# The first layer's modulation in five column blocks instead of four, with a half-width block at either end

## What is computed

```python
sc = jax.nn.silu(c)                 # latent tokens
scc = jax.nn.silu(c_ctx)            # context tokens
mod = sc @ ada_w + ada_b            # ada_w is 2048 x 6144
shift, scale, gate = jnp.split(mod[:, None, :], 3, axis=-1)
mod_c = scc @ ada_w + ada_b
h = rms_norm(x, norm_w) * (1 + scale) + shift
hc = rms_norm(ctx, norm_w) * (1 + scale_c) + shift_c
q, k, v, z = jnp.split(t @ w_in, 4, axis=-1)      # t is h, then hc; w_in is 2048 x 8192
```

## Time and profile before

| | us |
|---|---|
| median of 3 runs | 2140.7 (2139.47 to 2143.54) |
| the profiled execution's own time | 2139.08 |
| its span | 2137.5 |
| TensorE busy | 2049.5 (96%) |
| VectorE busy | 1438.1 (67%) |
| ScalarE busy | 913.5 |
| GpSimd busy | 776.6 |

### The profile page before, as it was taken

One profiled execution on the slowest core, in us unless ns is written; L12 is line 12 of the kernel. 1 busy time (PEld: TensorE's weight loads), 2 busy tenths in 40 slices (PEclk: granted clock), 3 DMA queues, 4 the chain that ended last, 5 costly groups with the idle time before them and its releaser, 6 DMA issues.

```text
span 2137.5 us, 31164 instructions
## 1 busy us (share of the span) xinstructions
PE 2049.5 (96%) x10694; PEld 1695.5 (79%) x10694; DVE 1438.1 (67%) x1865; ACT 913.5 (43%) x1259; POOL 776.6 (36%) x687
## 2 busy tenths in 40 slices
PE   5989999999999999989988999999999999999997
PEld 2558888888888888768867888888888888887776
DVE  5257777777787777744267767677767667678344
ACT  3244445444455455533354433433443434435433
POOL 1126666666665565645041221221322222222011
PEclk7999999999999999999989999999999999999999
DMA  9976666666676666445434455455454555544653
GB/s 352 361 218 143 184 162 170 171 175 176 174 189 171 169 174 171 137 133 152 111 106 123 127 138 148 118 137 149 106 162 113 142 141 134 127 133 167 239 194 138
DMA packets 417744, 349.21 MB, mean 163 GB/s; under 512 B 13504, under 2 KB 358176, under 8 KB 416544
## 3 DMA queue, kind: packets, MB, share of 16 engines
q1 hardware_dynamic: 392304, 269.76, 43.7%
q0 software_dynamic: 20400, 74.46, 13.8%
q10 hardware_dynamic: 4992, 4.37, 0.7%
HBM read 344.21 MB, written 4.33 MB: 163 GB/s over the span
## 4 chain that ended last, share of the span: by engine, by line
PE 84%; DVE 7%; DMA 3%; ACT 2%; issue 2%; POOL 0%; SPq 0%; DVEq 0%; POOLq 0%; ACTq 0%
PE bank L357 21%; PE bank L361 21%; PE bank L359 21%; PE bank L2104 2%; PE bank L2106 2%; PE bank L2105 2%; PE bank L2034 2%; DMA arena<-in_na_ada_w_dram 2%; DVE w_lo L343 2%; PE bank L2017 1%; PE bank L2027 1%; DVE act_lo L1513 1%; PE bank L1836 1%; PE bank L1810 1%; PE bank L1895 1%
## 5 line engine op out<-in xcount | busy, mean ns | idle before, releaser
L357 PE MATMUL bank<-act_hi,w_hi 128*128 128x512 f32 (+1 forms) x2480 | 916.6, 370 | 22.3 <-DVE w_lo L343 12.3
L361 PE MATMUL bank<-act_hi,w_lo 128*128 128x512 f32 (+1 forms) x2480 | 901.0, 363 | 0.0
L359 PE MATMUL bank<-act_lo,w_hi 128*128 128x512 f32 (+1 forms) x2480 | 900.9, 363 | 0.0
L343 DVE TENSOR_TENSOR w_lo<-arena,w_hi 128x2048 fp32r<-128x2048 f32 x186 | 441.7, 2375 | 182.7 <-ACT w_hi L339 132.7
L357 PEld LDWEIGHTS bank<-act_hi,w_hi 128*128 128x128 f32 x2480 | 471.1, 190 | 100.7 <-DVE w_lo L343 11.6
L361 PEld LDWEIGHTS bank<-act_hi,w_lo 128*128 128x128 f32 x2480 | 470.5, 190 | 73.8
L359 PEld LDWEIGHTS bank<-act_lo,w_hi 128*128 128x128 f32 x2480 | 471.4, 190 | 69.1
L581 POOL TENSOR_TENSOR acc<-acc,arena 128x512 f32<-128x512 f32 x224 | 334.1, 1492 | 123.0 <-ACT arena L830 113.9
L339 ACT ACTIVATE w_hi<-arena 128x2048 fp32r<-128x2048 f32 x141 | 269.2, 1909 | 97.7 <-PE bank L2106 78.2
L1316 DVE SCALAR_TENSOR_TENSOR arena<-arena,cond_c 128x512 f32<-128x512 f32 x240 | 253.3, 1056 | 72.8 <-DMA arena<-in_ssd_ada_w_dram 48.3
L830 ACT ACTIVATE arena<-arena,cond_c 128x512 f32<-128x512 f32 x256 | 171.3, 720 | 283.8 <-POOL acc L581 153.2
(11 more groups left out here) (247 smaller groups left out, 2123.4 us busy)
## 6 DMA issues: line engine op xcount, KB each, us to landing
arena<-in_ssd_w_in_dram SPq DMA_DIRECT2D x81, 1024.0 KB, 6.0
arena<-in_na_w_in_dram SPq DMA_DIRECT2D x58, 1024.0 KB, 7.2
arena<-in_ssd_ada_w_dram POOLq DMA_DIRECT2D x96, 512.0 KB, 4.1
arena<-in_na_ada_w_dram SPq DMA_DIRECT2D x64, 512.0 KB, 8.6
arena<-in_ssd_w_out_dram SPq DMA_DIRECT2D x32, 1024.0 KB, 5.0
arena<-in_na_ada_w_dram POOLq DMA_DIRECT2D x32, 512.0 KB, 4.1
arena<-in_na_w_out_dram SPq DMA_DIRECT2D x16, 1024.0 KB, 6.4
arena<-cs_scr SPq DMA_DIRECT2D x64, 256.0 KB, 5.3
```

The source lines that it names most:

```text
L343: nc.vector.tensor_tensor(w_lo[:, n0 % 2, :], raw[slot], w_hi[:, n0 % 2, :].bitcast(F32), ALU.subtract).then_inc(s_lo, 1)
L357: nc.tensor.matmul(bank[b][:, 0:cols], w_hi[:, b, w], act_hi3[:, k, 0:cols], start=(k == 0), stop=False)
L359: nc.tensor.matmul(bank[b][:, 0:cols], w_hi[:, b, w], act_lo3[:, k, 0:cols], start=False, stop=False)
L361: mm = nc.tensor.matmul(bank[b][:, 0:cols], w_lo[:, b, w], act_hi3[:, k, 0:cols], start=False, stop=(k == KT - 1))
```

## The change

The columns are taken in five blocks, given as first feature tile and number of tiles in `BLOCKS`: two tiles (256 columns), three times four, two. There are 40 steps instead of 32; those of the first and last block are two loads of 256 KB, in the same four slots. The weight groups keep their size and are loaded after q = 3 and q = 7 of the first four blocks; the last block has none among its steps.

The norm's row goes to bank 1 and is copied once to SBUF (`x_rows`); VectorE multiplies it onto tiles 0 and 1, and onto the other 14 only after the first block's `h`. The waits of the first block ask for two tiles only.

In TensorE's order the last block takes its first five steps before the first piece of the block ahead (`q >= 4 if c == 4`), three pieces come behind `mod_columns(4)`, and only four pieces are left at the end.

```diff
+BLOCKS = ((0, 2), (2, 4), (6, 4), (10, 4), (14, 2))
...
+            for c_block, (k0, kn) in enumerate(BLOCKS):
+                for q in range(8):
+                    n = 8 * c_block + q
+                    if n >= 4:
+                        sp.wait_ge(s_ada_used, n - 3)
+                    for b in range(2):
+                        sp.dma_start(ada_slot[n % 4][:, :, b, 0:P * kn],
+                                     ada_rows[:, 2 * q:2 * q + 2, b * D + P * k0:b * D + P * (k0 + kn)])\
+                          .then_inc(s_ada[n % 4], 16)
+                    if c_block < 4 and q % 4 == 3:
+                        load_first_weights(2 * c_block + q // 4)
...
-            pool.wait_ge(s_xn0, KT)
...
-            for k in range(KT):
-                nc.vector.tensor_tensor(xn_t[:, k, :], bank[3][:, :], xn_t[:, k, :], ALU.mult).then_inc(s_xn0, 1)
+
+            def x_normed(k0, k1):
+                for k in range(k0, k1):
+                    nc.vector.tensor_tensor(xn_t[:, k, :], x_rows, xn_t[:, k, :], ALU.mult).then_inc(s_xn0, 1)
+
+            step(nc.vector.tensor_copy(x_rows, bank[1][:, :]))
+            step.wait()
+            x_normed(0, BLOCKS[0][1])
...
+                if c == 0:
+                    x_normed(k0 + kn, KT)
...
-            for c in range(4):
+            for c in range(len(BLOCKS)):
+                pieces = [] if c == 0 else list(range(2 * BLOCKS[c - 1][1]))
                 for q in range(8):
                     mod_products(c, q)
                     if c == 0 and q == 2:
                         norm_rows()
-                    if c > 0 and q >= 2:
-                        first_tiles(c - 1, q - 2)
-                if c > 0:
-                    first_tiles(c - 1, 6)
+                    if q >= (4 if c == 4 else 2) and pieces:
+                        first_tiles(c - 1, pieces.pop(0))
+                if pieces:
+                    first_tiles(c - 1, pieces.pop(0))
                 mod_columns(c)
-                if c > 0:
-                    first_tiles(c - 1, 7)
-            for p in range(8):
-                first_tiles(3, p)
+                for p in pieces:
+                    first_tiles(c - 1, p)
+            for p in range(2 * BLOCKS[4][1]):
+                first_tiles(4, p)
```

More of the change, by code:

```diff
@@ L583, in _ @@
             for k in range(KT):
-                if k % 4 == 0:
-                    pool.wait_ge(s_mod, k // 4 + 1)
-                if k == KT - 4:
+                for c_block, (k0, kn) in enumerate(BLOCKS):
+                    if k == k0:
+                        pool.wait_ge(s_mod, c_block + 1)
+                        pool.wait_ge(s_xn0, k0 + kn if c_block == 0 else KT)
+                if k == BLOCKS[-1][0]:
                     load_ada(0, None, True)
@@ L788, in _ @@
             act.sem_inc(s_hi, PRE)
-            for c in range(4):
+            for c, (k0, kn) in enumerate(BLOCKS):
                 act.wait_ge(s_ada_used, 8 * (c + 1))
@@ L792, in _ @@
                     act.wait_ge(s_rtr, c)
-                nc.scalar.activation(rows_a[:, c % 2, :], bank[2][:, :], ACT.Copy).then_inc(s_rows, 1)
-                first_hi(2 * c)
+                nc.scalar.activation(rows_a[:, c % 2, 0:P * kn], bank[2][:, 0:P * kn], ACT.Copy).then_inc(s_rows, 1)
+                first_hi(k0 // 2)
                 act.wait_ge(s_mod, c + 1)
-                act.wait_ge(s_xn0, KT)
-                for k in range(4 * c, 4 * c + 4):
+                act.wait_ge(s_xn0, k0 + kn if c == 0 else KT)
+                for k in range(k0, k0 + kn):
                     h_high(k)
-                first_hi(2 * c + 1)
+                if kn > 2:
+                    first_hi(k0 // 2 + 1)
             def z_tanh_a(last):
@@ L1232, in first_lo @@
                                         w_hi[:, s % 2, 0:2 * PRE * P].bitcast(F32), ALU.subtract).then_inc(s_klo, 1)
-            for c in range(4):
+            for c, (k0, kn) in enumerate(BLOCKS):
                 dve.wait_ge(s_rtr, c + 1)
                 modulation(c)
[L1237 to L1240, removed]
+                if c < 2:
+                    dve.wait_ge(s_xn0, k0 + kn if c == 0 else KT)
+                first_lo(k0 // 2)
+                for k in range(k0, k0 + kn):
                     if k >= 3:
@@ L1796, in norm_rows @@
                 for t in range(4):
-                    mm = nc.tensor.matmul(bank[3][:, t * P:(t + 1) * P], ones[:, :], diag_x[:, t, :],
+                    mm = nc.tensor.matmul(bank[1][:, t * P:(t + 1) * P], ones[:, :], diag_x[:, t, :],
                                           start=True, stop=True)
@@ L1818, in mod_columns @@
                     pe.wait_ge(s_mod, c)
-                else:
-                    pe.wait_ge(s_xn0, KT)
-                for m in range(4):
+                for m in range(BLOCKS[c][1]):
                     mm = nc.tensor.matmul(bank[3][:, 4 * m:4 * m + 4], rows_a[:, c % 2, m * P:(m + 1) * P],
@@ L1841, in first_tiles @@
                         mm.then_inc(s_pre, 1)
-                if p % 4 == 3 and k < KT - 1:
+                if kk == 1 and p % 2 == 1 and k < KT - 1:
                     mm.then_inc(s_kused, 1)
-            for c in range(4):
+            for c in range(len(BLOCKS)):
+                pieces = [] if c == 0 else list(range(2 * BLOCKS[c - 1][1]))
                 for q in range(8):
```

37 lines of the change are left out of this document (15 added, 22 removed).

## The result

| | before | after |
|---|---|---|
| median of 5 runs, us | 2142.55 (2139.47 to 2144.56) | 2151.8 (2150.42 to 2154.93) |
| ratio, 95% interval | | 1.0052 (1.0041 to 1.0062) |
| the profiled execution's own time | 2139.08 | 2150.42 |
| its span | 2137.5 | 2148.8 |

The changed kernel is slower: by 9.3 us in the medians of the table, by 11.1 if the ratio is taken (0.52% of 2140), and by 11.3 between the two profiled spans. The forecast was 2144.7 with a range up to 2150: the time lies above the range.

The account below looks back on a forecast made before the run. TensorE and DMA were taken as both full, their paces per block equal within 1%. 2.4 at `turn_values`, 1.3 clock and 0.3 behind it sum to +4.0: 2144.7 us against the median; forecast's own range 2142 to 2147.5, all terms 2139.5 to 2150.

Parts of the forecast that it names:

- half steps: Half-width loads of block 0: each costs between 1.36 and 1.60 us, taken as 1.45.
- step 8: First step of block 1: lands at 38.0 plus 1.0 for landings falling behind their bytes, so 39.0.
- a norm that nothing waits for: Norm ahead of and behind the first block's `h`: 14 multiplications, 8.5 us, moved behind it on VectorE; cost 0.
- step 20: Start of block 3's products: lands at 78.7; TensorE would be there at 77.4 and waits 1.3.
- the start of the last block: TensorE takes up the last block at 123.3, late, since its first four steps have landed by about 118.
- a wait for slot 0: Last block's fifth product: slot freed only at 123.9, loads landed at 128.3, a new wait of 2.6.
- `turn_values`: Its first start, after the last block's pieces: 156.7 against 154.33, +2.4 before the clock's term.
- the clock's 1.3: TensorE's clock falls again ahead of step 18: +1.3 us, 0 if it does not, 2.8 if nothing covers it.
- The rule of the Trainium skill: DMA loads: fixed 2 us plus bytes, so batch to 1 MiB; by its fit a half step 2.2, sum 3 us higher.
- slow refill: Rival, last block: the slot freed at 123.9 lands after 8.6 instead of 4.1, +4.5 on top, 2149.2; chance 0.13.
- cost per load: Rival, first and last block: a load costs per load, not per byte, half steps at 2.71, +7.8, 2148.5; chance 0.07.
- Behind it: After the first `turn_values`: later loads make TensorE wait 1.7 in `scores`, mostly absorbed by its 2.83 wait; +0.3 (0 to 2).

Follow-up runs that it names:

- parts_early: Changed kernel with the gate's first two parts loaded, multiplied and added between the last full block's `h` and the last block, from own buffers; ratio 1.0028 to the kernel before.
- bias_early: Changed kernel with only the first head's bias table (loads and addition on GpSimd) moved ahead of the last block's `h`; ratio 1.0037 to the kernel before.
- norm_only: Kernel before, its four full blocks kept, with the norm's part of the change alone; ratio 0.9994.
- before_late_pool: Kernel before with six additions of unused result on GpSimd behind its last `h`; ratio 1.0001.
- start_half: Changed kernel with blocks of 2, 2, 4, 4, 4 tiles, the second half-width block moved to the start, pieces from q = 2; ratio 1.0061 to the kernel before.

## Why the prediction was wrong

**Right, by its own steps.** Block 0's last product at 33.93 (forecast 32.9), half steps 1.47 apart (1.45), step 8 at 38.78 (39.0), a norm that nothing waits for, the lower clock in block 2 (66.7 to 76.9, forecast 66 to 76), step 20 at 80.41 (78.7; without the short wait forecast there), the start of the last block at 124.85 (123.3), a wait for slot 0 of 2.29 (2.6), the wait for `h` gone, `turn_values` at 157.17 (158.0 with the clock). I had added the clock's 1.3 at the end; put where it lies, ahead of step 20, it makes these starts 80.0 and 124.6, within 0.4. The last block's four products then took 1.93 instead of 2.4, which is most of what is left: +2.8 at `turn_values`, against +3.7. The rule of the Trainium skill that I weighed (DMA: Bandwidth & Descriptors: batch to 1 MiB in the section Bandwidth; the fit with a fixed 2 us stands in the section Anatomy of one DMA — SWDGE (gpsimd) path, and is measured for loads issued from GpSimd, while these are SyncE's) did not show as a price here: a half step of two 256 KB loads came 1.47 after the last, 0.54 of 2.71, where an estimate by that fit has 0.81. I had also priced it too high: three half steps at 2.2 instead of 1.45 are 2.3 us, not 3. The two rivals that hung on loads, slow refill and cost per load, did not come about.

**The step that failed** is the term "Behind it", +0.3 (0 to 2). I followed the late loads along VectorE to the first head's q and k, found a TensorE wait of 2.83 that could absorb them, and stopped. It did absorb them: that wait is 2.83 again. The lateness was not gone, it went on in GpSimd's queue, where the bias table stands behind the gate's parts, and came out one and two heads later, as a wait of 2.2 and stretches of lower clock: +7.1 in the profile where the term had at most 2. parts_early and bias_early show it, since moving the parts or the table leaves 0.2 and 1.2 of the 7.1. I had the row of VectorE's parts, but of GpSimd's queue only the two loads, and never asked when the last instruction of that queue is due.

How much of the 7 is this lateness, in time? One stretch of 1.7 near 160 is also in the profiles of the other four four-block kernels, though not in that of before. norm_only, which has it, grows by 1.5 from the first to the third head; set against that, the growth is 5.6. Of the time at the third head 4.0 is gone again by the start of the last stage, 3.3 of it by where the stretches of lower clock between 900 and 1300 happen to lie. parts_early is 0.0024 lower in the ratio (5.1 us), but half of what its profile gains lies in the last stage.

**Not foreseen at all** is the last stage: +5.3 in the profile, for which the sum, which ends at the first head, has no term. About 2 of it are waits that go with the place of an instruction fetch, in profiles and once in medians; the rest is lower clock, a part of it the luck of the kernel before in its one profile.

Between the profiled spans the account is closed: +2.9 at the first head, +7.1 by the third, -4.0 from there to the last stage, +5.3 in it, together 11.3. Of the 9.3 us of the medians (11 by the ratio) some 3 are what the prediction had; how the rest divides between the queue behind the last `h` and the last stage the runs don't fix. No version that computes everything beats the kernel before; norm_only equals it, and parts_early is the best of them with five blocks.

## What to carry to other kernels

When the end of a stage is cut, list every engine's queue that stands behind that end, down to the last instruction that anyone waits for, and compare its new due time with the new start of the consumer: here TensorE's first visible wait took up the lateness of one queue, and another queue's came out 35 us later. Cover that a cut removes is a cost with a size of its own: here 12.9 us had hidden the preparation, and 9.0 did not. And where a resource is exactly full (26.34 of TensorE against 26.5 of DMA per block), a shorter start and a shorter end only move idle time into the middle.

## What the runs showed of the hardware

- An instruction fetch of one packet (0.02 MB, 0.4% of the engines' time in its stretch) beside crowded loads went with a wait for these loads of 7.9 to 8.5 us (three profiles) instead of 6.6 to 7.3 (four), and with a load of 2 MB that landed after 10.5 to 11.0 instead of 9.2 to 9.8. 32 matmuls added 1.9 ms earlier brought it in or took it out. That the fetch is the cause is not shown.
- A load's size cost by its bytes in a full queue: 1.47 for two loads of 256 KB, 2.71 for two of 512 KB.
- TensorE's clock fell for 3.4 us after single waits of 2.2 to 2.8 in three places of the changed kernel, and did not after a wait of 3.0 in parts_early (1.00 from 160 to 166). The same wait of 2.8 to 2.9 near 160 had a fall behind it in four of the five four-block kernels and none in the kernel before: whether such a stretch of 1.7 us comes is not settled by the length of the wait.
- GpSimd's pair of additions (128x512) took 4.62 in the changed kernel and 3.02 before. The 4.62 is in before_late_pool too, where the pair only starts 2.5 later (148.91 instead of 146.45), so it does not come from the five blocks; start_half has 3.03. What beside it decides, no run separates.
